# Starting each tile's dense stages one period sooner, and giving the number picking a period of its own

## What is computed

```
n = rms_norm(h, g_mix);  proj = n @ w_in
o = concat(gated_delta_net(...), sliding_window_attention(...))   # 8 heads each
h1 = h + o @ w_out
xn = rms_norm(h1, g_ffn)
s1, s2 = scores of xn @ w_query against two sets of 128 keys, 8 heads
v1, i1 = top_k(s1, 16);  v2, i2 = top_k(s2, 16)
cand = v1[:, None] + v2[None, :]                 # 16 x 16 per head
sc, ci = top_k(cand, 16)
eid = take(i1, ci // 16) * 128 + take(i2, ci % 16)    # "picking the numbers"
gate = softmax(sc)
hid = einsum(expert_u[eid], xn)                  # 128 rows of 1024 per token
h2 = h1 + einsum(gelu(hid) * gate, expert_v[eid])
out = h2 + sigmoid(rms_norm(h2, g_ple) @ w_gate) * (p @ w_proj)
```

## Time and profile before

| What | Value |
|---|---|
| runs, median (lowest, highest) | 3554.31 us (3550.28, 3556.14) |
| profiled execution | 3553.76 us |
| its span, first to last instruction | 3552.0 us |
| mean granted TensorE clock | 0.871 |
| busy: PE, DVE, ACT, POOL | 2597.7, 2229.9, 1169.4, 2134.8 us (73, 63, 33, 60%) |
| moved by DMA | 1229.39 MB, mean 346 GB/s; gathers 1073.87 MB |
| first expert dot product of tile 0, 1, 2, 3 | 323.9, 897.5, 1269.0, 1641.6 us |

### The profile page before, as it was taken

How to read it: one execution, slowest core, us unless ns; L and a number is a source line. 1 busy time by engine, 2 the same in 40 slices (tenths; PEclk the granted TensorE clock), 3 DMA queues, 4 the chain that set the end, 5 groups by cost and what they waited for, 6 DMA issues and landing times.

```text
span 3552.0 us, 37526 instructions
## 1 busy us (share of the span) xinstructions
PE 2597.7 (73%) x10985; PEld 1197.2 (34%) x10985; DVE 2229.9 (63%) x7062; ACT 1169.4 (33%) x3402; POOL 2134.8 (60%) x2069
## 2 busy tenths in 40 slices
PE   7996895775678667865786577757776677657877
PEld 5653342531343124321432143214421343213322
DVE  3124564567766866686668667777677766845543
ACT  2321233332343233323342234223422342223332
POOL 2202343445776677766777677767766777667663
PEclk9998997897889888977988798889898889778888
DMA  8115787788999999999999999999999999999995
GB/s 298 59 47 203 240 302 283 277 294 334 394 393 391 385 388 393 391 396 386 396 382 406 376 395 385 405 381 390 397 393 384 386 398 394 387 398 381 377 369 213
DMA packets 379092, 1229.39 MB, mean 346 GB/s; under 512 B 36313, under 2 KB 65545, under 8 KB 378761
## 3 DMA queue, kind: packets, MB, share of 16 engines
q0 software_dynamic: 294912, 1073.87, 78.1%
q1 hardware_dynamic: 80920, 143.51, 11.1%
q10 hardware_dynamic: 3056, 9.63, 0.7%
HBM read 1203.87 MB, written 22.99 MB: 345 GB/s over the span
## 4 chain that ended last, share of the span: by engine, by line
PE 32%; DMA 18%; issue 17%; POOL 17%; DVE 11%; ACT 5%; SPq 0%; POOLq 0%; DVEq 0%; ACTq 0%
PE bank L1111 16%; PE expert_sum L1111 15%; DMA v_rows<-in_peer_v_dram,expert_id 13%; POOL u_rows L659 9%; POOL v_rows L668 8%; DMA u_rows<-in_peer_u_dram,expert_id 4%; DVE u_rows L2010 4%; PE bank L1114 2%; ACT L698 1%; ACT weight_diagonals L698 1%; DMA w_query<-in_w_in_dram 1%; DVE arena L1957 1%; DVE arena L1963 1%; DVE arena L1966 1%; ACT arena L698 1%
## 5 line engine op out<-in xcount | busy, mean ns | idle before, releaser
L1111 PE MATMUL expert_sum<-v_rows,weight_diagonals 128*64 128x512 f32 x4096 | 1179.9, 709 | 585.7 <-issue 441.8
L2010 DVE CUSTOM_DVE_ANT_0 u_rows<-u_rows,ffn_in 128x512 f32<-128x512 f32 x2048 | 1308.2, 686 | 345.1 <-DMA u_rows<-in_peer_u_dram,expert_id 343.8
L659 POOL DMA_INDIRECT u_rows<-in_peer_u_dram,expert_id x1024 | 1044.5, 1020 | 665.8 <-issue 390.0
L668 POOL DMA_INDIRECT v_rows<-in_peer_v_dram,expert_id x1024 | 1041.9, 1017 | 537.2 <-issue 288.9
L1111 PEld LDWEIGHTS expert_sum<-v_rows,weight_diagonals 128*64 128x64 f32 x4096 | 318.7, 156 | 1263.1 <-issue 1252.5
L1111 PE MATMUL bank<-w_query,arena 128*128 128x512 f32 x576 | 281.3, 636 | 34.8 <-DMA w_query<-in_peer_w_query_dram 33.8
L698 ACT ACTIVATE weight_diagonals<-constants,expert_weight 128x64 f32<-128x64 f32 x1024 | 272.5, 336 | 8.3
L1111 PE MATMUL bank<-arena 128*128 128x128 f32 (+4 forms) x2176 | 251.2, 286 | 26.1 <-DVE arena L1770 12.1
L1111 PEld LDWEIGHTS bank<-arena 128*128 128x128 f32 (+3 forms) x2176 | 234.2, 193 | 81.6 <-issue 49.9
L1114 PE MATMUL bank<-constants,arena 128*128 128x128 f32 x952 | 149.1, 298 | 117.9 <-DVE arena L1810 40.6
L1111 PE MATMUL bank<-w_out_sb,arena 128*128 128x512 f32 x512 | 226.7, 599 | 9.5 <-ACT arena L1077 6.3
(11 more groups left out here) (193 smaller groups left out, 2053.9 us busy)
## 6 DMA issues: line engine op xcount, KB each, us to landing
w_query<-in_peer_w_query_dram SPq DMA_DIRECT2D x64, 1024.0 KB, 12.3
u_rows<-in_peer_u_dram,expert_id POOLq DMA_INDIRECT x1024, 7.6
v_rows<-in_peer_v_dram,expert_id POOLq DMA_INDIRECT x1024, 7.5
w_out_sb<-in_w_out_dram SPq DMA_DIRECT2D x2, 4096.0 KB, 20.6
w_query<-in_w_in_dram SPq DMA_DIRECT2D x12, 512.0 KB, 7.7
conv_scratch<-w_query SPq DMA_DIRECT2D x12, 448.0 KB, 6.6
arena<-conv_scratch SPq DMA_DIRECT2D x7, 768.0 KB, 5.0
tok_scratch<-token_out ACTq DMA_DIRECT2D x7, 648.0 KB, 2.9
```

The lines of the kernel that those rows point to most:

```text
L659: nc.gpsimd.indirect_dma_start(u_ring[:, j, :], None, table_u, bass.IndirectOffsetOnAxis(id_of(q, j), 0)).then_inc(u_landed[j], 16)
L668: nc.gpsimd.indirect_dma_start(v_ring[:, j, :], None, table_v, bass.IndirectOffsetOnAxis(id_of(q, j), 0)).then_inc(v_landed[j], 16)
L1111: return nc.tensor.matmul(out_, lhsT, rhs, start=start, stop=stop, **kw)
L2010: last = v.tensor_tensor_reduce(u_ring[:, j, half], u_ring[:, j, half], xb[:, j % NB, half], 1.0, 0.0, ALU.mult, ALU.add, hid_half[:, q % ...
```

## The change

The lists get 17 pieces. `piece1` becomes a piece of its own and runs in period 15, one tile ahead; piece 0 and the decays both run in period 0; everything up to `best_pair(1)` then comes one period sooner. The first pick gets a period of its own (11), `best_pair(2)` and `best_pair(3)` stay in 12 and 13, the latter now alone, and the second pick stays in 14. In `pick`, `fill(1)` stands after each of the six large steps. On TensorE `add_h1` leaves the generator `expert_slots` and stands at the head of period 1, since `piece2` of the next front now runs in that period. On ScalarE and TensorE the lists shift in the same way. In tile 0 only the first pick moves, from period 13 to 12.

```
--- before.py
+++ after.py
@@ -442,9 +442,14 @@
         def front_piece(q):
 
             e, g = divmod(q, NG)
-            if e == 0:
-                return {6: (0, 1), 7: (2, 3), 8: (4, 5), 9: (6, 7), 10: (8, 9), 11: (10,), 12: (11,), 13: (12, 13), 14: (14,)}.get(g, ())
-            return (g,) if e < NT - 1 and g < NG - 1 else ()
+            if e == 0 and g < NG - 1:
+                at = {6: (0, 1, 2), 7: (3, 4), 8: (5, 6), 9: (7, 8), 10: (9, 10), 11: (11,), 12: (12, 13), 13: (14, 15), 14: (16,)}
+                return [(1, i) for i in at.get(g, ())]
+            if g == NG - 1:
+                return [(e + 2, 1)] if e + 2 < NT else []
+            if e == NT - 1:
+                return []
+            return [(e + 1, 0), (e + 1, 2)] if g == 0 else [(e + 1, g + 2)]
 
         def w_channel(ct):
 
@@ -957,11 +962,11 @@
                 act.wait_ge(gate_arg, 1 if cols.stop == EARLY * G else t + 2)
                 f(gate_new[:, cols], gate_new[:, cols], ACT.Exp).then_inc(gate_exp, 1)
 
-            pieces = [lambda t: (piece0(t), piece1(t)), decays_of, lambda t: (piece2(t), piece3(t)),
+            pieces = [piece0, piece1, decays_of, lambda t: (piece2(t), piece3(t)),
                       lambda t: (level(t, 1), level(t, 2)), lambda t: (level(t, 3), level(t, 4)), piece6,
                       lambda t: (attention_norm(t), piece8(t)), lambda t: (piece9(t), piece10(t)),
                       lambda t: (piece11(t), piece12(t)), lambda t: (normed_T(t), query_pair(t, 0)),
-                      lambda t: query_pair(t, 1), lambda t: query_pair(t, 2), lambda t: query_pair(t, 3),
+                      lambda t: query_pair(t, 1), lambda t: query_pair(t, 2), lambda t: None, lambda t: query_pair(t, 3),
                       lambda t: None, piece_gate]
 
             def take_ids(t, n, cols):
@@ -1011,7 +1016,7 @@
 
 
             first, rest, whole = slice(0, EARLY * G), slice(EARLY * G, SLOTS), slice(0, SLOTS)
-            for piece in pieces[:9]:
+            for piece in pieces[:10]:
                 piece(0)
             normed_T(0)
             for pair in range(2):
@@ -1051,8 +1056,8 @@
                 if q == 2:
                     take_ids(0, 2, rest)
                     take_gates(0, 2, rest)
-                for i in front_piece(q):
-                    pieces[i](q // NG + 1)
+                for e, i in front_piece(q):
+                    pieces[i](e)
                 if q % NG == NG - 2:
                     take_ids(q // NG + 1, q // NG + 3, whole)
                     take_gates(q // NG + 1, q // NG + 3, whole)
@@ -1419,11 +1424,11 @@
                     last = mm(to_s[:, s * P:s * P + P], qrT[:, s, :], keysT[:, 4 * pair + s, :])
                 last.then_inc(score_mm, 1)
 
-            pieces = [piece0, piece1, lambda t: (piece2(t), piece3(t)), lambda t: (level(t, 1), level(t, 2)),
+            pieces = [piece0, lambda t: None, piece1, lambda t: (piece2(t), piece3(t)), lambda t: (level(t, 1), level(t, 2)),
                       lambda t: (level(t, 3), level(t, 4)), lambda t: (piece6(t), piece7(t, 0), piece7(t, 1)), piece8,
                       lambda t: (piece9(t), piece10(t)), lambda t: (piece11(t), project_out(1)),
                       lambda t: (piece12(t), query_pair(t, 0)), lambda t: query_pair(t, 1), lambda t: query_pair(t, 2),
-                      lambda t: query_pair(t, 3), lambda t: None, lambda t: None]
+                      lambda t: None, lambda t: query_pair(t, 3), lambda t: None, lambda t: None]
 
             def add_h1(t):
 
@@ -1471,9 +1476,7 @@
 
             def expert_slots(q):
 
-                t, g = divmod(q, NG)
-                if g == 0:
-                    add_h1(t)
+                g = q % NG
                 for pair in range(PAIRS):
                     for b in range(NB):
                         pe.wait_ge(v_landed[pair * NB + b], (q + 1) * 16)
@@ -1502,7 +1505,7 @@
                     pass
 
             first, rest, whole = slice(0, EARLY * G), slice(EARLY * G, SLOTS), slice(0, SLOTS)
-            for piece in pieces[:11]:
+            for piece in pieces[:12]:
                 piece(0)
             finish_slots()
             rows_to_pairs(0)
@@ -1518,12 +1521,14 @@
                 t = q // NG + 1
                 slots = expert_slots(q - 1) if q else iter(())
                 credit = 0
+                if q % NG == 1:
+                    add_h1(t - 1)
                 for ct in channel_tiles(q):
                     channels(ct)
                 if q % NG == NG - 1:
                     rows_to_pairs(t)
-                for i in front_piece(q):
-                    pieces[i](t)
+                for e, i in front_piece(q):
+                    pieces[i](e)
                 finish_slots()
                 if q == 2:
                     ids_to_pairs(3, rest)
@@ -1571,6 +1576,8 @@
             pe.wait_ge(vector_front, NT)
             for g in range(NG):
                 slots = expert_slots((NT - 1) * NG + g - 1)
+                if g == 1:
+                    add_h1(NT - 1)
                 finish_slots()
                 if g == 1:
                     pe.wait_ge(c_w_loaded, 32)
@@ -1677,6 +1684,7 @@
                     x_inverses(1, 2)
 
             def piece1(t):
+                fill(4 if t > 1 else 0)
                 projected(dve, t, 1)
                 if t == 0:
                     dve.wait_ge(params_b, 16 * 4)
@@ -1958,13 +1966,16 @@
                                     cst[:, C_IOTA:C_IOTA + TOPK].unsqueeze(1).broadcast_to([P, nh * TOPK, TOPK]),
                                     chalf_f[:, half, cols].unsqueeze(2).broadcast_to([P, nh * TOPK, TOPK]),
                                     ALU.is_equal).then_inc(vector_step, 1)
+                    fill(1)
                     dve.wait_ge(vector_step, steps(t))
                     by_half = key_numbers.rearrange("p (h f) k -> p f h k", f=2)[:, half]
                     v.tensor_tensor(onehot[:, 0:nh], onehot[:, 0:nh], by_half.unsqueeze(2).broadcast_to([P, nh, TOPK, TOPK]),
                                     ALU.mult).then_inc(vector_step, 1)
+                    fill(1)
                     dve.wait_ge(vector_step, steps(t))
                     v.reduce_sum(e_half[:, half, cols], onehot[:, 0:nh].rearrange("p h k a -> p (h k) a"),
                                  AX.X).then_inc(vector_step, 1)
+                    fill(1)
                     dve.wait_ge(vector_step, steps(t))
 
                 if t:
@@ -1988,12 +1999,13 @@
                 dve.wait_ge(vector_step, steps(t))
                 v.tensor_tensor(by_head, by_head, per_head(g_inv[:, h0:h1], h1 - h0, TOPK), ALU.mult).then_inc(signal_done, 1)
 
-            pieces = [lambda t: (piece0(t), piece1(t)), decays_of, lambda t: (piece2(t), piece3(t)),
+            pieces = [piece0, piece1, decays_of, lambda t: (piece2(t), piece3(t)),
                       lambda t: (level(t, 1), level(t, 2)), lambda t: (level(t, 3), level(t, 4)),
                       lambda t: (level(t, 5), piece7(t, 0), piece7(t, 1)), lambda t: (attention_norm(t), piece8(t)),
                       lambda t: (piece9(t), piece10(t)), lambda t: (residual(t, 0), residual(t, 1), piece12(t)),
-                      lambda t: None, lambda t: best_pair(t, 0), lambda t: best_pair(t, 1), lambda t: best_pair(t, 2),
-                      lambda t: (best_pair(t, 3), pick(t, 0, 4)), lambda t: (pick(t, 4, 4), gates(t, 0, PH, vector_front))]
+                      lambda t: None, lambda t: best_pair(t, 0), lambda t: best_pair(t, 1), lambda t: pick(t, 0, 4),
+                      lambda t: best_pair(t, 2), lambda t: best_pair(t, 3),
+                      lambda t: (pick(t, 4, 4), gates(t, 0, PH, vector_front))]
 
             def expert_dots(q):
                 e, g = divmod(q, NG)
@@ -2041,12 +2053,12 @@
                     v.tensor_copy(h2_sb[:, n * 512:n * 512 + 512], acc[:, n * 512:n * 512 + 512]).then_inc(h2_ready, 1)
 
 
-            for i, piece in enumerate(pieces[:10]):
-                if i == 3:
+            for i, piece in enumerate(pieces[:11]):
+                if i == 4:
                     x_inverses(3, 2)
-                elif i == 5:
+                elif i == 6:
                     x_inverses(5, 2)
-                elif i == 7:
+                elif i == 8:
                     x_inverses(7, 1)
                 piece(0)
             best_pair(0, 0)
```

48 lines of the change are left out of this document (29 added, 19 removed).

## The result

| | before | changed |
|---|---|---|
| median | 3553.8 us | 3578.26 us |
| lowest, highest | 3546.58, 3557.03 us (7 runs) | 3572.1, 3591.39 us (7 runs) |
| span of the profiled execution, clock | 3552.0 us, 0.871 | 3576.4 us, 0.868 |

The ratio is 1.008, 95% interval 1.0068 to 1.0091. Forecast were 3551 us, range 3531 to 3569: the time lies 9 us above the range, and by sign and size nearest to rival C (3579), whose mechanism didn't occur.

A forecast was written before the change was run, and what follows sets the result against it. DMA engines bound it at some 390 GB/s, with a hole each tile where VectorE's picking stops GpSimd's gathers. Terms -28 - 7 + 32 = -3 us from 3554.3 gave 3551 us, range 3531 to 3569.

The forecast's parts named there:

- rival C: Picking, periods 13 and 14: smoothing doesn't close the hole, since dots inside the pick find no rows landed; 3579, chance 0.05.
- (c): Earlier start: chain of copies, add_h1 and scalings in period 1 stops GpSimd; 5.3 us a tile, +32 us, bounds 0 to +54.
- (a): Picking, periods 13 and 14: both GpSimd stops go, 4.7 us in each of tiles 1 to 6, -28 us.
- rival A: Period 1: the stop is mostly covered by queued gathers; 3551 - 12 to 3551 - 30, centre 3534, chance 0.28.
- (b): Tile 0's crowded last stages: first pick one period ahead returns part of the stops; -7 us, bounds -3 and -10.
- Rival B: Period 1: chain starts over 2.7 us late behind TensorE's v products; 2 to 3 us more a tile, 3566, chance 0.22.
- the reserve that was forecast there: Periods 0 and 1: TensorE's last v group for period 15 done at 19.0, 2.7 us before experts_out needs it.
- D: Picking: large pick steps hold up GpSimd's issues beside them, 7.4 us a tile; up to +44, 3595, chance 0.04.
- (d): Tile end: ids for the next tile's u gathers come later but with cover of about 10 us; costs nothing.
- (e): SP's queue: loads and the sum's store shift with the pieces, no other queue is passed; costs nothing.

The follow-up runs named there:

- e9: Kernel before plus three dot products on VectorE ahead of piece2's wait for add_h1 (the cover): 3530.5 us, 0.9945 of the kernel before.
- e13: Changed kernel with the three dot products ahead of piece2's wait and the picking taken back to its old order, without dots: 3549.42 us, 1.0003 of the kernel before.
- e11: Changed kernel with three dot products ahead of piece2's wait, without the dots between the picking's steps: 3549.94 us, 0.9997 of the kernel before.
- e7: Changed kernel plus three dot products on VectorE ahead of piece2's wait for add_h1: 3535.77 us, 0.9954 of the kernel before.
- e5: Changed kernel run again with nothing edited, on another chip: 3579.97 us, 1.0077 of the kernel before.
- e10: Kernel before with dot products between the picking's steps and nothing else, on a normal chip: 3552.24 us, 1.0002 of the kernel before.
- e15: Kernel before with three dot products ahead of piece2's scalings and three between the picking's steps: 3534.41 us, 0.996 of the kernel before.
- e16: Changed kernel with three dot products ahead of piece2's wait and VLAG 4, a run of 8 v gathers instead of 12: 3719.78 us, 1.0482 of the kernel before.
- e17: Changed kernel with three dot products ahead of piece2's wait and VLAG 7, a run of 14 v gathers instead of 12: 3592.82 us, 1.0129 of the kernel before.
- e8: Changed kernel, three dots ahead of piece2's wait, all six period-15 dots ahead of piece 1, ScalarE copying rows first: 3539.62 us, 0.9965 of the kernel before.
- e14: Changed kernel with three dot products ahead of piece2's wait and piece 1 back in period 0: 3589.46 us, 1.011 of the kernel before.
- e1: Kernel before with dot products between the picking's steps and nothing else, on the slow chip: 3957.17 us, 0.9992 of the kernel before there.
- e2: Changed kernel without the dot products between the picking's steps, on the slow chip: 3941.28 us, 0.9946 of the kernel before there.

## Why the prediction was wrong, step by step

**What failed** is the size of term (c), the earlier start. The prediction put it at 5.3 us a tile, +32 us; the ledger has 9.6 a tile, 58 us. The other terms were less wrong: the picking was to give 28 us and gives 29 at its place, of which part is lost in period 15, and tile 0 was to give 7 and gives 2.9.

The runs form a path as well, in medians on the normal chips: 3551.5 before; -21 the cover (e9, 3530.5); +19 the earlier start (e13); +0.5 the period of its own (e11); -14 the dots in the picking (e7, 3535.8); +44 the cover taken away: 3580 (e5). Steps under 8 us are within the intervals. Read this way, and if the cover is worth the same with the old and the new picking, which no run shows, the earlier start without cover costs -21 + 19 + 44 = 42 us and the picking's two changes give 14, tile 0 included. Either way of dividing the miss has (c) too cheap; by the path (a) was also put at twice its worth.

**(a) The picking: the term right at its place, wrong as a gain.** Forecast 4.7 us a tile, the ledger shows 4.8 less, no stop in periods 13 and 14, rate 409 in period 14. But period 15, some 20 us later, loses 2.0 more than before (1.0 by the second profiles). GpSimd has only v gathers left at the end of a tile, since the u gathers of the next wait for its numbers; it goes round the ring of eight v slots as fast as these land and TensorE uses them. The landing (minimum, median, maximum) of the v gathers issued from 33 to 22 us ahead of tile 4's first dot product, kernel before (1980 to 1991 us):

```profile
DMA to landing us min/median/max: 6.9/7.3/7.6
```

and changed kernel (1995 to 2006 us):

```profile
DMA to landing us min/median/max: 12.9/13.9/15.4
```

The waits of GpSimd in that period, changed kernel:

```profile
2006.51 0.94 POOL L673 DMA_INDIRECT v_rows<-in_peer_v_dram,expert_id  x1 [3.07 <-PE expert_sum L1116]
...
2013.81 1.41 POOL L673 DMA_INDIRECT v_rows<-in_peer_v_dram,expert_id  x1 [5.13 <-PE expert_sum L1116]
```

It looks as if, with no hole in front of it, the queue were full when the ring of v becomes the supply. In the old schedule e10 and e15 show the exchange: the picking's dots take 1.3 from periods 13 and 14 and put 1.8 and 1.7 into 15. In the changed schedule it is the own period that does so (e13 to e11: -3.3 and +3.2), while the dots then take 2.7 off period 15 again (e11 to e7). And the earlier start alone, with the hole of the picking still there (e13), has 1.6 more in period 15 than e9, and landings as long as the changed kernel's: the medians of the v gathers issued 35 to 20 us ahead of the next tile are, over tiles 1 to 5, 7.5 to 8.5 us in the kernel before, 12.2 to 14.1 in e10, 12.5 to 14.1 in e13, 13.9 to 14.5 in the changed kernel. So the missing hole isn't needed for long landings. Nor do long landings and stops set the loss: e11 has landings like e7's (13.5 to 15.4 us against 13.3 to 15.5), stops for v slots that sum to less (9.8 us a tile against 11.5 over tiles 1 to 5), and loses twice as much. e16 fits the landing time as the cause, e17 does not. What sets period 15's loss stays open; e8 and e14 show only that piece 1 and the tokens have no part in it. The prediction had the deep queue only as an argument for rival A.

**(b) Tile 0: same mechanism, over-sized.** Forecast -7, measured -2.9. Period 14 there began at 840.79 instead of 844.63, the 3.8 us of the forecast, and the stops fell from 19.89 and 6.64 us to 11.00 and none. Then the v burst waited, 8.19 us in one piece where it was 1.57:

```profile
882.98 0.97 POOL L673 DMA_INDIRECT v_rows<-in_peer_v_dram,expert_id  x1 [8.19 <-PE expert_sum L1116]
```

**(c) The earlier start: the step that failed, by its size.** The chain was named rightly, place and order, here in tile 4: copies to 23.0 us into the tile (measured 25.0), `add_h1` to 26.9 (28.9), scalings to 31.6 (33.4), first dots to 34.1 (35.9). It ran 2 us late throughout, because period 0 ended at 21.3 instead of 19.2 (20.0 to 21.4 over the tiles of both profiles). "About 2 of waits" was the part that was too small: VectorE waited 4.3 us there (3.0 to 4.4), 2.8 of them in front of the decays' second product, since on TensorE a group of v products stood before it and took 3.68 us, at a granted clock of 0.50, instead of 1.94:

```profile
2040.63 3.68 PE L1116 MATMUL expert_sum<-v_rows,weight_diagonals 128*64 128x512 f32 x8
2044.24 1.36 PE L1116 MATMUL bank<-arena,constants 128*128 128x512 f32 x2
```

```profile
2045.63 0.69 DVE L1727 TENSOR_TENSOR arena<-bank,small 128x512 f32<-128x512 f32 x1 [2.79 <-PE bank L1116]
```

The first stop followed, 7.15 us where 5.1 were forecast; the second was 4.52 instead of 2.3, since from the last scaling to the products of keys passed 5.2 us, where I had 3.75, and behind these stand 3.4 us of L1758 to L1766 before the next dot. Stops 11.7 us instead of 7.4, and with a cover of 3 to 4 us they cost what period 1 shows, some 7.5 a tile more than before, where 4.7 were forecast. Two terms were missing: +1.6 in period 0, whose front is longer now (that this is the reason is not shown), and +2.0 in period 15, part of it from (a). Set against these, periods 6 to 12 improved by 1.9, not forecast either. In all (c) had +5.3 a tile and the ledger, without the picking's row, has +9.6: 58 us instead of 32. The bound of +54 was near that; the range left it out.

**Rival B** had the side and part of the mechanism. A v group at half the clock did make the chain late, but through the decays of period 0: VectorE's copies never stood idle for TensorE's last group, in no tile of either profile, so the reserve that was forecast there held. Its price of 2 to 3 us a tile gave 3566; 4.3 more than the forecast were needed. **Rival A** fails in its cause: the stops were not covered by queued work. **C**: the dots inside the pick found their rows. **D**: GpSimd's twelve issues beside the pick took 12.65 us, 1.05 each against 0.94 undisturbed, 1.3 us in 16, and the rate stayed at 409. The Trainium skill (SBUF - State Buffer, the box on DVE blocking DMA) has GpSimd's descriptor writing locked out while a VectorE instruction in a two-port mode holds the port pair they share. Whether any of the pick's steps holds it, no run here shows; this window has at most that tenth, and no cost.

**(d) and (e).** The numbers were in time: GpSimd came to the first u gather of tile 4 at 2020.92 and waited 0.30 us. "Nothing" for SP's queue holds for the time only. The tokens' load took SP 5.50 us to issue (4.9 to 6.1 in the tiles of the changed kernel) instead of 0.75, and piece 1 had them only at 2011.55:

```profile
2011.55 0.17 DVE L1691 TENSOR_TENSOR small<-arena,dt_bias_rows 128x8 f32<-128x8 f32 x1 [10.50 <-DMA arena<-tok_scratch]
```

e8 shows that this wait costs nothing.

## What to carry to other kernels

A transfer-bound loop with a software queue loses wherever the feeding engine meets a dependent chain through another engine. Before a piece is moved ahead, count the independent work left to stand in that chain at its new place: three dot products in front of one wait were worth 44 us in the moved schedule and 21 in the old one. A hole that is filled can reappear a period later; take a gain at one place as gross until the ledger of the whole loop, in windows summed per stage, has been made again. And try the cheap fill in the old schedule first: the kernel before with that one line (3530.5 us) equals the changed one with it (3535.8) and beats both kernels of this study.

## Not expected of the hardware

Chips differ by more than the change: the kernel before takes 3550 to 3554 us on every chip but one, and 3964 on that, where the granted clock is 0.83 instead of 0.87; in e1 TensorE's idle time without a visible releaser in L1111's front matmuls is 175 us there. The order of the variants seems to change with it: without the picking's dots the change gains 0.5% there (e2), while on normal chips the changed kernel loses 0.8% and e11, which has the cover as well, gains nothing. v gathers took 13.9 us to land in period 15 of the changed kernel, 7.3 in the kernel before at the same place; and one DMA issue of SP, the tokens' load, grew from 0.75 to 5.50 us there.
